# MLP up blocks in halves of 256 features, with one 512-column product for top and rest

## What is computed

```python
# first block
h2 = rmsnorm(x, g_mlp_pre[l])
y = jnp.square(jax.nn.relu(h2 @ w_up[l])) @ w_down[l]
x = x + rmsnorm(y, g_mlp_post[l])
# second block
def _sq_relu_mlp(u, w1, w2):
    return jnp.square(jax.nn.relu(u @ w1)) @ w2
# w_up, w_mlp1: (2048, 8192); w_down, w_mlp2: (8192, 2048)
```

## Time and profile before

| | |
|---|---|
| median of 3 runs | 2642.36 us (2642.03 to 2643.64) |
| profiled execution, first to last instruction | 2641.5 us |
| PE busy | 2615.6 us, 99% |
| DVE busy | 1858.9 us, 70% |
| ACT busy | 1333.3 us, 50% |
| POOL busy | 283.5 us, 11% |
| DMA | 572.30 MB, mean 217 GB/s |

### The profile page before, as it was taken

The page is one execution under the profiler, slowest core; times in us unless marked ns, Lnnn a source line. Parts: engine busy times, 40 slices in busy tenths (PEclk is TensorE's granted clock), DMA queues, the critical chain, the costliest instruction groups (busy, mean ns, idle before and its releaser), DMA issues.

```text
span 2641.5 us, 42197 instructions
## 1 busy us (share of the span) xinstructions
PE 2615.6 (99%) x17850; PEld 2376.8 (90%) x17850; DVE 1858.9 (70%) x2235; ACT 1333.3 (50%) x1785; POOL 283.5 (11%) x257
## 2 busy tenths in 40 slices
PE   9999999999999999999999999999999999999998
PEld 8888976998998988988999899999799898998997
DVE  5555665899999777787678866677555675446555
ACT  5455553554444444466874346666454444443444
POOL 1332321010000000000010311120000000000011
PEclk9999999999999999999999999999999999999999
DMA  9645454668687888876566744446657786555553
GB/s 321 179 144 160 152 172 147 210 250 303 249 294 277 287 310 296 293 265 214 159 215 240 269 133 148 145 154 217 209 172 249 252 301 211 188 183 193 189 191 128
DMA packets 287339, 572.30 MB, mean 217 GB/s; under 512 B 9846, under 2 KB 29073, under 8 KB 286704
## 3 DMA queue, kind: packets, MB, share of 16 engines
q1 hardware_dynamic: 281456, 548.69, 60.9%
q0 software_dynamic: 5696, 20.92, 2.8%
HBM read 565.78 MB, written 3.27 MB: 215 GB/s over the span
## 4 chain that ended last, share of the span: by engine, by line
PE 95%; DVE 2%; ACT 1%; DMA 0%; issue 0%; SPq 0%; POOL 0%; ACTq 0%; DVEq 0%
PE p_gemm L2218 51%; PE p_gemm L2267 32%; PE p_gemm L2244 3%; PE p_b L2462 1%; PE p_gemm L2280 1%; PE p_b L2493 1%; DVE w_lo L1268 1%; PE p_b L2660 1%; ACT w_hi L707 1%; PE p_b L2669 1%; PE p_b L2556 1%; PE p_b L2313 0%; PE p_gemm L2237 0%; DMA w_raw<-in_w_in 0%; PE p_b L2476 0%
## 5 line engine op out<-in xcount | busy, mean ns | idle before, releaser
L1268 DVE TENSOR_TENSOR w_lo<-w_raw,w_hi 128x1024 fp32r<-128x1024 f32 (+1 forms) x864 | 1063.6, 1235 | 668.6 <-ACT w_hi L707 667.5
L707 ACT ACTIVATE w_hi<-w_raw 128x1024 fp32r<-128x1024 f32 (+1 forms) x864 | 897.2, 1040 | 1175.5 <-PE p_gemm L2218 665.4
L2218 PE MATMUL p_gemm<-h_hi,w_hi 128*128 128x256 f32 x2920 | 828.2, 284 | 4.6 <-DVE w_lo L1268 1.9
L2218 PE MATMUL p_gemm<-h_lo,w_hi 128*128 128x256 f32 x2920 | 820.3, 281 | 0.0
L2218 PE MATMUL p_gemm<-h_hi,w_lo 128*128 128x256 f32 x2920 | 820.2, 281 | 0.0
L2218 PEld LDWEIGHTS p_gemm<-h_hi,w_hi 128*128 128x128 f32 x2920 | 550.1, 188 | 14.2 <-issue 5.7
L2218 PEld LDWEIGHTS p_gemm<-h_lo,w_hi 128*128 128x128 f32 x2920 | 550.3, 188 | 0.9
L2218 PEld LDWEIGHTS p_gemm<-h_hi,w_lo 128*128 128x128 f32 x2920 | 550.2, 188 | 0.0
L2267 PE MATMUL p_gemm<-w_hi,a_hi 128*128 128x512 f32 x1008 | 393.1, 390 | 0.0
L2267 PE MATMUL p_gemm<-w_hi,a_lo 128*128 128x512 f32 x1008 | 392.4, 389 | 0.0
L2267 PE MATMUL p_gemm<-w_lo,a_hi 128*128 128x512 f32 x1008 | 392.2, 389 | 0.0
(11 more groups left out here) (433 smaller groups left out, 2505.8 us busy)
## 6 DMA issues: line engine op xcount, KB each, us to landing
w_raw<-in_w_mlp SPq DMA_DIRECT2D x128, 1024.0 KB, 5.1
w_raw<-in_w_in SPq DMA_DIRECT2D x107, 1024.0 KB, 5.3
ada_w<-in_w_ada SPq DMA_DIRECT2D x96, 1024.0 KB, 6.1
w_raw<-in_w_up SPq DMA_DIRECT2D x64, 1024.0 KB, 9.0
w_raw<-in_w_down SPq DMA_DIRECT2D x64, 1024.0 KB, 9.2
w_raw<-in_w_out SPq DMA_DIRECT2D x32, 1024.0 KB, 5.1
w_raw<-in_w_in SPq DMA_DIRECT2D x36, 768.0 KB, 4.8
cmp_w<-in_phi_w POOLq DMA_DIRECT2D x2, 2048.0 KB, 14.9
```

The source lines that it names most:

```text
L707: act.activation(WH[:, s % 4, :, 0:n], RAW[:, s // 2, 2 * (s % 2):2 * (s % 2) + 2, 0:n], ACT.Copy)\
L1268: dve.tensor_tensor(WL[:, s % 4, :, 0:n], RAW[:, s // 2, 2 * (s % 2):2 * (s % 2) + 2, 0:n], WH[:, s % 4, :, 0:n].bitcast(F32), ALU.subtrac ...
L2218: ins = pe.matmul(dst, w[:, s % 4, kk, cols], x[:, k, :], start=k == 0 and m % 2 == 0 and i == 0, stop=k == KC - 1 and i == 2, skip_group_ ...
```

## The change

Of the 32 up blocks 30 are "halved" (all but 16 and 76, the first of each MLP). A halved block is made as two halves of 256 features, half 0 in units 0 to 3 and G[0], half 1 in units 4 to 7 and G[1]; a unit holds four chunks k of two pieces m. The host reorders the columns and rows of `w_up` and `w_mlp1` so that a unit's weights lie as before, and DMAs, roundings and rests stay the same. `h_hi` and `h_lo` become one tile, with the top's 256 columns and the rest's 256 columns side by side, so one product of 512 columns takes both against the rounded weights; its left half sums the tops, its right half the rests. The weight rest's product (256 columns) is added to the right half.

Out of PSUM the two halves have to be added: ACT copies the left part into R2 and the right part into `up_rest` (a tile that lies where `a_lo` does), in slots 3 and 7; POOL adds them, per half; ACT makes the ReLU of all 1024 columns in slot 0 of the next block; POOL squares it. Rounding and rest of the hidden layer move from slot 1 to slot 2. The PSUM buffer of every block is counted anew, and blocks 16 and 76 use G[1] in place of G[0]. Two pairs of semaphores are merged to make room.

```diff
+UP_BLOCKS = [b0 + GB * g + q for b0 in (B_MLP1, B_MLP2) for g in range(GROUPS) for q in range(4)]
+HALVED = [b for b in UP_BLOCKS if b not in (B_MLP1, B_MLP2)]
-        HH = at("h_hi", H0, [P, KC, T], F32R)
-        HL = at("h_lo", H0 + 16 * K, [P, KC, T], F32R)
+        HHL = at("h_hi_lo", H0, [P, KC, 2, T], F32R)
+        HH, HL = HHL[:, :, 0, :], HHL[:, :, 1, :]
+        UPR = at("up_rest", A0 + 32 * K, [P, KC, T])
...
+            def half_sum(b, half):
+                pool.wait_ge(*gemm_read(b, half))
+                part = R2[:, 2 * half:2 * half + 2, :]
+                pool.tensor_tensor(part, part, rest_part(b, half), ALU.add).then_inc(S("up_sum"), 1)
             def mlp_squares(b0):
                 for q in range(4):
-                    pool.wait_ge(*gemm_read(b0 + q))
+                    b = b0 + q
+                    if b in HALVED:
+                        half_sum(b, 0)
+                        half_sum(b, 1)
+                        pool.wait_ge(S("up_positive"), halved_before(b) + 1)
+                    else:
+                        pool.wait_ge(*gemm_read(b))
                     pool.tensor_tensor(R2[:, :, :], R2[:, :, :], R2[:, :, :], ALU.mult).then_inc(S("relu2_ready"), 1)
...
+            def half_out(b, half):
+                act.wait_ge(S("unit_used"), count(b, None, UPB, UPB // 2 * (half + 1)))
+                act.wait_ge(S("act_lo"), UP_BLOCKS.index(b))
+                act.activation(R2[:, 2 * half:2 * half + 2, :], G[half][:, :, 0:T], ACT.Copy)
+                act.activation(rest_part(b, half), G[half][:, :, T:2 * T], ACT.Copy).then_inc(gemm_read(b, half)[0], 1)
+            def relu_sum(b):
+                act.wait_ge(S("up_sum"), 2 * halved_before(b) + 2)
+                act.activation(R2[:, :, :], R2[:, :, :], ACT.Relu).then_inc(S("up_positive"), 1)
+            def up_out(b0, acts0, q, s):
+                b = b0 + q
+                if s == 0 and b - 1 in HALVED:
+                    relu_sum(b - 1)
+                if s == 2 and 1 <= q <= 4:
+                    relu_rounded(acts0, q)
+                if s % 4 == 3 and b in HALVED:
+                    half_out(b, s // 4)
+                if s == UPB - 1 and q < 4 and b not in HALVED:
+                    relu(b0, acts0, q)
...
-                        if s == 1 and 1 <= q <= 4:
+                        if s == 2 and 1 <= q <= 4:
                             relu_rest(acts0, q)
...
+            def up_unit(b, s):
+                half = s // 4
+                if s % 4 == 0:
+                    pe.wait_ge(*gemm_free(b, half))
+                pe.wait_ge(S("lo_ready"), count(b, None, UPB, s + 1))
+                for i in range(2):
+                    for z in range(2):
+                        k = 4 * (s % 4) + 2 * i + z
+                        for m in range(2):
+                            cols = slice(T * z + P * m, T * z + P * m + P)
+                            pe.matmul(G[half][:, m, :], WH[:, s % 4, i, cols], HHL[:, k, :, :].rearrange("p z t -> p (z t)"),
+                                      start=k == 0, stop=False, skip_group_check=True)
+                            ins = pe.matmul(G[half][:, m, T:2 * T], WL[:, s % 4, i, cols], HH[:, k, :],
+                                            start=False, stop=k == KC - 1, skip_group_check=True)
+                ins.then_inc(S("unit_used"), 1)
...
             def mlp_block(b, q, s, acts0, ready=None):
-                if q < 4:
+                if b in HALVED:
+                    up_unit(b, s)
+                elif q < 4:
                     gemm_unit(b, None, s, HH, HL, ready)
```

More of the change, by code:

```diff
@@ L85, with psum_uses @@
 GB = 8
+UP_BLOCKS = [b0 + GB * g + q for b0 in (B_MLP1, B_MLP2) for g in range(GROUPS) for q in range(4)]
+HALVED = [b for b in UP_BLOCKS if b not in (B_MLP1, B_MLP2)]
+def psum_uses():
+    uses, n = {}, [0, 0]
+    for b in range(N_BLOCKS):
+        for half in range(2 if b in HALVED else 1):
+            buf = half if b in HALVED else 1 if b in UP_BLOCKS else b % 2
+            n[buf] += 1
+            uses[b, half] = (buf, n[buf])
+    return uses
+PSUM_USES = psum_uses()
 def block_chunks(b):
@@ L345, in quad, with gemm_read, gemm_free, rest_part @@
             return t[:, 4 * q:4 * q + 4, :]
-        def gemm_read(b, g=None):
-            n = b // 2 + 1
-            return S(f"gemm_read{b % 2}"), (n if g is None else g * (GB // 2) + n)
+        def gemm_read(b, half=0):
+            buf, n = PSUM_USES[b, half]
+            return S(f"gemm_read{buf}"), n
+        def gemm_free(b, half=0):
+            buf, n = PSUM_USES[b, half]
+            return S(f"gemm_read{buf}"), n - 1
+        def rest_part(b, half):
+            c = 4 * (UP_BLOCKS.index(b) % 4) + 2 * half
+            return UPR[:, c:c + 2, :]
+        def halved_before(b):
+            return len([h for h in HALVED if h < b])
         PAIRS = [(k, r) for k in ("slc", "win", "cmp", "dil", "fox", "moba") for r in range(4)]
@@ L832, in _ @@
                 if s == S_GELU:
-                    act.wait_ge(S("gelu_arg"), 1)
-                    act.activation(GT[:, 2, :], GT[:, 1, :], ACT.Exp, scale=-1.0).then_inc(S("gelu_exp"), 1)
+                    act.wait_ge(S("gelu_ready"), 1)
+                    act.activation(GT[:, 2, :], GT[:, 1, :], ACT.Exp, scale=-1.0).then_inc(S("gate_exp"), 1)
                     act.wait_ge(S("misc_nat"), 1)
@@ L934, in relu @@
             def relu(b0, acts0, q):
-                act.wait_ge(S("unit_used"), count(b0 + q + 1, None, UPB))
+                b = b0 + q
+                act.wait_ge(S("unit_used"), count(b + 1, None, UPB))
                 act.wait_ge(S("act_lo"), acts0 + q)
-                act.activation(R2[:, :, :], gview(q % 2), ACT.Relu).then_inc(gemm_read(q)[0], 1)
+                act.activation(R2[:, :, :], gview(1), ACT.Relu).then_inc(gemm_read(b)[0], 1)
+            def half_out(b, half):
[7 more added lines that the diff above has]
+            def up_out(b0, acts0, q, s):
+                b = b0 + q
+                if s == 0 and b - 1 in HALVED:
[6 more added lines that the diff above has]
+                    relu(b0, acts0, q)
             def down_copy(b, m):
@@ L982, in _ @@
                             scale_x0(s - 2, STD0)
-                        if s == 1 and 1 <= q <= 4:
-                            relu_rounded(acts0, q)
-                        if s == UPB - 1 and q < 4:
-                            relu(b0, acts0, q)
+                        up_out(b0, acts0, q, s)
                         if g == GROUPS - 2 and q >= 4 and s == 3:
@@ L2185, in bank, with gemm_buf @@
                 return PB[i]
+            def gemm_buf(b):
+                return PSUM_USES[b, 0][0]
+            def up_unit(b, s):
[13 more added lines that the diff above has]
+                ins.then_inc(S("unit_used"), 1)
             def gemm_half(b, g, s, kk, top, rest, ready=None):
@@ L2192, in gemm_half @@
                         pe.wait_ge(S(ready[0]), ready[1] + s + 1)
-                    if s == 0 and (g is not None or b >= 2):
-                        pe.wait_ge(*gemm_read(b - 2, g))
+                    if s == 0 and b >= 2:
+                        pe.wait_ge(*gemm_free(b))
                     if b == 0 and s == 0:
@@ L2213, in gemm_half @@
                 for m in range(n):
-                    dst = gview(b % 2)[:, m, :]
+                    dst = gview(gemm_buf(b))[:, m, :]
                     cols = slice(P * m, P * m + P)
@@ L2408, in compress_turn @@
             def compress_turn():
-                pe.wait_ge(S("gelu_ready"), 1)
+                pe.wait_ge(S("gelu_ready"), 2)
                 ps = bank(CMP_BANKS[0], "cmp_read", 2)
@@ L2828, with in_halves @@
     w_out_2 = np.concatenate([x["w_out_2"][0][HGW:], x["w_out_2"][0][:HGW]], 0)
+    def in_halves(w, b0):
+        w = w.copy()
+        blocks = [b0 + GB * g + q for g in range(GROUPS) for q in range(4)]
+        for i, b in enumerate(blocks):
+            if b in HALVED:
+                tile = w[:, 512 * i:512 * i + 512].reshape(KC // 2, 2, P, 2, T)
+                w[:, 512 * i:512 * i + 512] = tile.transpose(3, 0, 2, 1, 4).reshape(D, 512)
+        return w
     prm = np.zeros((P, NPRM), f)
```

14 lines of the change are left out of this document (7 added, 7 removed).

## The result

The kernel after takes 2649.5 us, the median of 8 runs (2648.1 to 2653.0), beside 2642.5 (2642.0 to 2644.4) for the kernel before in the same session: a ratio of 1.0028, with a 95% interval of 1.0020 to 1.0037. It is slower by 7 us. I had forecast 2640.3 and no difference that can be measured; the time lies inside my range (2623 to 2652), on the other side of zero.

The account below looks back on a forecast made before the run. PE bounds the kernel, busy 2615.6 of 2641.5 us, with DVE next in line. From 2642.4, less 18.9 for products, plus 15.1 for waits and 1.7 for clock, gives 2640.3 us; range 2623 to 2652.

Parts of the forecast that it names:

- The waits: At the four ada products in blocks 18, 20, 26, 28, PE waits 15.1 us for DVE, each POOL sum costing DVE 1.04.
- The rival in which the sums don't hold DVE: POOL's sums don't slow DVE, or its lateness never reaches PE; 2623.4 us, chance 0.15.
- The mutual wait of ACT and DVE: In blocks 17 to 19 and 24 to 27 each engine delays the other, 1.2 us a block; 2648.7 us, chance 0.08.
- ACT's ReLU against the square: Before the late ada products, ACT's new ReLU delays the operand 0.95 us; POOL's square no longer stops DVE (1.64); set equal.
- The pair: In 30 up blocks, one 512-column product replacing two of 256 saves PE 9.87 ns, 18.9 us in all.
- the rival of the costlier pair: In every up block, wide plus narrow product costs more than 345.1 ns; 2655.5 us if nothing is saved, chance 0.15.
- the sign that I had named for it: Second MLP's up blocks taking 22.5 us or more, in place of the forecast 22.1, would show the product saving wrong.
- The clock: After PE's waits of about 5 us at blocks 20 and 28, the lowered clock loses 0.85 us each, 1.7 together.
- The "0.9 us around the span": Difference between profiled span 2641.5 and median 2642.4 us before the change, taken as untouched by it.
- The rest at nothing: ACT's 2.4 us more a block, later hidden-layer steps, PSUM buffers and weight DMAs outside the late stretches cost nothing.

## Why the prediction was right and wrong

**The waits: right.** Place (blocks 18, 20, 26, 28), cause (1.04 us of DVE for each sum) and size (15.1 predicted, 12.6 idle and 13.7 from start to start) held. Without the sums they are gone, without the halves in the two full groups too. The rival in which the sums don't hold DVE falls by the 1.78 us row. The mutual wait of ACT and DVE is there but small: where that rival has 8.4 us, DVE's waits for `w_hi` grew from 0.5 to 1.2 and from 0.9 to 2.0 us. ACT's ReLU against the square I had set equal; in block 20 they are 1.18 + 0.86 = 2.0 us against 1.64, so 0.4 us were missing there.

**The pair: the step that failed.** "I take 9.87, from rows of the same stages" priced the wide product by the down blocks, at 226.80 ns. There weights move and a is stationary; here h moves, and it takes 233 ns behind its like, and a pair 346.7 or 353.3 in place of 345.1. The term 1920 x 9.87 = 18.9 us measured 1920 x 5.0 = 9.6: the mechanism was there, its size was half. Its error of 9.3 us is by itself as large as the distance from forecast to median, 9.2. It is the rival of the costlier pair; its formula gives 2642.4 + 13.1 - 1.54 x 5.0 = 2647.8, and x = 5.0 is just past the 5.1 below which I had put "slower". Of the sign that I had named for it, 22.5 us or more for an up block of the second MLP, the trace shows both sides: 353.3 ns a pair make 22.6 us a block in 77 to 79, 346.7 make 22.2 in 92 to 95. I gave that rival 0.15, although showed that the same product takes 118.3 or 120.0 ns depending on its tiles. I mentioned that row and then didn't ask what differs between these tiles; the answer, the place in SBUF, would have opened the question of where a 512-column h begins. The place accounts for a part only; what else makes the wide product of h dearer than that of weights stays open. By the Trainium skill, "TensorE: Matmul & The Clock Gate", section "Wait — 56ns, not 53.3ns?", a product costs about 2.5 ns beyond its columns, and an estimate from this figure is 4.8 us for the 1920 pairs. The measured 9.6 agrees with neither that estimate nor my rows.

**The clock: mis-sized in the profiled run.** I took 1.7 us, half of what the earlier trace rows allowed (3.4); the profiled run lost 4.9. For the median run the subtraction above leaves 2.9 for all that is not pairs or waits, so there the error is about 1 us. The two long waits were 4.4 us, not 2.6, and the low stretch behind them was longer: 4.7 and 5.9 us of work at 1.2 GHz, and that beyond what fell into the wait itself (1.7 us of the window 590 to 593). My two errors past the pair, 3.2 too little here and 1.4 too much in the waits, add 1.8 us to the profiled run, which was itself slower than the median by 3.5. The "0.9 us around the span" was no such thing: it set the span of one run against the median of others. For the profiled run of the kernel after, time and span differ by 1.8 us (2652.97 and 2651.2). No term of the sum rested on it.

**The rest at nothing: held.** The copies, the later ReLU and the moved slots cost nothing where DVE has room: from block 32 on no wait of PE is new, and the second MLP gained 5.2 us.

**What the change is worth.** The two kernels with h at 32 differ by the 23 halved blocks alone: 2631.28 to 2626.20, 5.1 us, where 1472 pairs at 346.9 ns in the mean in place of three products at 116.7 (350.0) make 4.6. Moving h by 64 bytes, with the small tiles behind it, gives 11.1 us in the kernel before, more than twice as much. The best kernel here has both and is 0.63% faster than before.

## What to carry to other kernels

Price a new product by rows in which the same operand moves and the same one stands still, from the same place in SBUF; where rows of one shape differ by 1 or 2%, find out why before counting in thousands of them. When a change adds POOL work with two SBUF inputs, look where DVE has no gap and leave that stretch as it was. Here a wait of PE of 4.4 us cost its length and then 2.2 or 2.7 us of clock.
